# Expert down product of a decoder layer: both halves of the contraction as split products, with GpSimd making the low part of the second half

## The chip, the cores and the metric

The kernel runs on one core of a Trainium2 chip. The metric is the device time of one execution in microseconds. Times come from runs of the same program on the chip, and the rows below come from one further execution that was profiled.

## The reference

One decoder layer for 512 tokens of width 1024 in float32. It has a token mixer (a state-space branch and windowed attention, merged by gates, and an output product), and after it a mixture of experts, which is where the change lies:

```python
h2 = rmsnorm(x, norm_ffn)
gates = ...                      # top-1 of 4 groups, top-2 of its 4 experts: 16 experts in all
gu = jnp.einsum('nd,edf->nef', t, w_up)        # per expert: 1024 -> 512
g_part, u_part = jnp.split(gu, 2, axis=-1)
act = jax.nn.silu(g_part) * u_part * gates[..., None]
out = jnp.einsum('nef,efd->nd', act, w_down)   # per expert: 256 -> 1024
x = x + out
```

## The kernel before

Up to about 346 us of the profiled span the mixer and the router run. Then come the 16 experts, one after another. For each expert the kernel holds a list of up to 128 tokens. GpSimd gathers their rows from HBM (`gather`, line 674), TensorE transposes them (`turn_rows`, 2086), multiplies them by the up weights (`up`, 2100 to 2102), ScalarE and VectorE form the activation, TensorE transposes it (`turn_act`, 2112) and multiplies it by the down weights (`down_`). ScalarE scales the result by the token's gate out of PSUM (`rows_out`, 1011), and GpSimd adds the rows to the output in HBM with an accumulating indirect DMA (`add_rows`, 698; for the last four experts in two halves, 687).

Most products are split products. A float32 operand is written as a high part, which is rounded to `float32r` by a ScalarE copy, and a low part, the float32 operand less its high part, which VectorE computes. The product is then three `float32r` matmuls: high by high, high by low, low by high. The up product is split in full: 8 chunks of the contraction, three matmuls each, on two half weights (`high_up` at 977, `low_up` at 1596). The down product has a contraction of 256, that is two chunks `k`. Chunk 0 is split (2126 to 2128); its down weights get their high part on ScalarE (`high_down`, 997) and their low part on VectorE (`low_down`, 1642), its activations likewise (`turned_act` at 990, `low_act` at 1646). Chunk 1 is a plain float32 matmul (2121) from the unsplit activations (copied at 989) and the weights as they were loaded. The output has two column halves `h` of 512, each in its own PSUM bank.

The order on each engine is written out by hand. With `e` the expert whose up product is running:

- TensorE: up product of e, in the first six steps the small products that place two further token lists (2073), transposes of the activations of e-1, transposes of the rows of e+1, down product of e-1. In a down product the plain matmuls of both halves come first, then the three split matmuls of each half. The last expert's half 0 is finished before half 1 is begun.
- ScalarE: high part of the first up half of e+1, rows out of e-2, high down weights of e-1, high part of the second up half of e+1 (which waits until three halves back is used), transposed activations of e-1, tanh for e, high part of the rows of e+1.
- VectorE: list work (1578 to 1591) in the first steps, low part of the first up half of e+1, low down weights of e-1, low part of the second up half of e+1, low activations of e-1, low part of the rows of e+1 (1630), the activation of e (1636, 1638).
- GpSimd: gathers run ahead; before the gather of expert e comes the add of expert e-5. The gather of e waits until the rows of e-2 have been transposed. An add waits for the rows out of its own expert and for the landing of the add before it.
- SyncE loads up halves into a ring of 12 and down weights into 4 slots, expert e+3 after the down product of e-1 is done.

Of the kernel before, what the change touches and what calls it, by code (L numbers as in the profile page):

```python
# [6 lines left out]
F32 = mybir.dt.float32  # L7
# [17 lines left out]
def hybrid_layer(nc, x, norm_mix, w_in, lam_re, lam_im, log_dt, b_re, b_im, c_re, c_im, d_skip,  # L25
# [36 lines left out]
    with ExitStack() as ctx:  # L62
# [3 lines left out]
        def sem(name):  # L66
# [8 lines left out]
                     att=3 * 1024, v=TT * KW, kt=KVH * SEQ, rot=4 * SPC * CH // 2, ssm=max(SSM_FLOATS, 4 * DOWN + 6 * 256))  # L75
# [99 lines left out]
        at_high = [rounded(f"at_high{i}", "att", 1280 + 2 * D + 256 * i, [P, P]) for i in range(2)]  # L175
        at_low = [rounded(f"at_low{i}", "att", 1792 + 2 * D + P * i, [P, P]) for i in range(2)]
        dn_high = [rounded("dn_high", "att", 0, [P, D])] * (NE - 1) + [rounded("dn_high_last", "ga", 0, [P, D])]
        dn_low = [rounded(f"dn_low{s}", "ssm", s * DOWN, [P, D]) for s in range(4)]
# [126 lines left out]
        dn_high_done, dn_low_done, at_low_done = (sem(n) for n in ("dn_high_done", "dn_low_done", "at_low_done"))  # L305

# [288 lines left out]
        def _(g):  # L595
# [105 lines left out]

            for t in range(TT):
                g.wait_ge(h2_stored[t], 16)
            for e in range(NE):
                if e == 5:
                    g.wait_ge(x2_stored, 16 * TT)
                if e >= 5:
                    add_rows(e - 5)
                if e < 2:
                    g.wait_ge(first_idx, e + 1)  # L710
                elif e in LISTS:
                    g.wait_ge(idx_done, LISTS.index(e) + 1)
                gather(e)
            for e in range(NE - 5, NE):
                add_rows(e)

# [16 lines left out]
        def _(act):  # L733
# [252 lines left out]
            def turned_act(e):  # L986

                act.wait_ge(at_full, e + 1)
                act.activation(actT[e % 2][:, 1, :], sc[1][:, P:2 * P], ACT.Copy).then_inc(at_done, 1)
                act.activation(at_high[e % 2][:], sc[1][:, 0:P], ACT.Copy).then_inc(at_done, 1)  # L990

            def high_down(e):
# [4 lines left out]
                act.activation(dn_high[e][:], down[e % 4][:, 0, :], ACT.Copy).then_inc(dn_high_done, 1)  # L997
# [63 lines left out]
        def _(v):  # L1061
# [578 lines left out]
            def low_down(e):  # L1640
                v.wait_ge(dn_high_done, e + 1)
                tt(dn_low[e % 4][:], down[e % 4][:, 0, :], dn_high[e][:].bitcast(F32), ALU.subtract).then_inc(dn_low_done, 1)

            def low_act(e):
                v.wait_ge(at_done, 2 * (e + 1))
                tt(at_low[e % 2][:], sc[1][:, 0:P], at_high[e % 2][:].bitcast(F32), ALU.subtract).then_inc(at_low_done, 1)
# [50 lines left out]
        def _(pe):  # L1697
# [417 lines left out]
            def down_(e):  # L2115
                pe.wait_ge(at_done, 2 * e + 1)
                pe.wait_ge(down_loaded[e % 4], 16 * (e // 4 + 1))
                cols = [slice(h * 512, (h + 1) * 512) for h in range(2)]

                def plain(h):  # L2120
# [105 lines left out]
```

## Time and profile before

| | us |
|---|---|
| median of 3 runs | 535.05 |
| lowest and highest | 531.87, 536.57 |
| the profiled execution | 533.41 |
| its span in the trace | 531.6 |
| TensorE busy | 503.6 (95%) |
| VectorE busy | 385.2 (72%) |
| ScalarE busy | 296.8 (56%) |
| GpSimd busy | 146.7 (28%) |

PE is TensorE's matmuls, PEld its weight loads, DVE is VectorE, ACT is ScalarE, POOL is GpSimd. L with a number is a line of the kernel. Positions are microseconds from the start of the span. The names `arena_front` and `arena_back` are two large SBUF tensors in which most tiles lie, so a tile's name in a row is often that of the arena; the line says which it is. `m_both` are the two PSUM banks of the down product, `sc_both` holds the transposed activations, `tp` the transposed rows and, for the last expert, the down product.

### The profile page before, as it was taken

Reading aid. Unit: us, or ns where it says so; the run is one execution under the profiler, and the core shown is the slowest. Engines: PE = TensorE matmul, PEld = TensorE weight load, DVE = VectorE, ACT = ScalarE, POOL = GpSimd, SP = SyncE. Lnnn points to the kernel's source line nnn. Section 1 sums busy time; section 2 is a strip of 40 time slices with the busy share of each in tenths; the row PEclk is TensorE's granted clock in tenths of the full one; section 3 lists DMA queues with packets and bytes.
Section 4 is the critical chain, followed back from the end, with each engine's and each line's share of the span. In section 5 each row is a group of like instructions: output and inputs, shape, how many; then the busy total and the mean of one; then the engine's idle time right before and its main releaser. Section 6 shows DMA issues by size and latency. Waiting matters only on the chain.

```text
span 531.6 us, 7304 instructions
## 1 busy us (share of the span) xinstructions
PE 503.6 (95%) x2610; PEld 409.4 (77%) x2610; DVE 385.2 (72%) x609; ACT 296.8 (56%) x523; POOL 146.7 (28%) x188
## 2 busy tenths in 40 slices
PE   6999999898999999999999999779999999999992
PEld 4988787687777887778888888777878877777761
DVE  4889876989879658665758424578988888788740
ACT  6635143776676876632335102345677777787741
POOL 1229429294470000000000000032233223345344
PEclk9999999999999999999999999958999999999997
DMA  8660460222012220243587547579999999966433
GB/s 312 85 206 1 121 197 5 76 80 80 27 54 80 61 60 0 60 118 103 174 297 284 232 188 287 193 247 413 370 322 338 321 357 372 331 234 175 123 46 38
DMA packets 62774, 93.93 MB, mean 177 GB/s; under 512 B 14183, under 2 KB 45959, under 8 KB 62738
## 3 DMA queue, kind: packets, MB, share of 16 engines
q1 hardware_dynamic: 56304, 80.84, 44.2%
q0 software_dynamic: 5184, 8.41, 7.3%
q10 hardware_dynamic: 1250, 4.22, 2.0%
q8 instruction: 21, 0.34, 0.3%
q14 instruction: 15, 0.12, 0.1%
HBM read 88.19 MB, written 12.58 MB: 190 GB/s over the span
## 4 chain that ended last, share of the span: by engine, by line
PE 82%; DVE 9%; ACT 4%; DMA 2%; issue 1%; POOL 0%; SPq 0%; POOLq 0%; DVEq 0%; ACTq 0%
PE pj L1723 12%; PE pj L1725 11%; PE pj L1724 11%; PE pj L2100 6%; PE pj L2101 6%; PE pj L2102 6%; PE m_both L2121 5%; PE tp L2086 3%; DMA arena_front<-in_w_in_dram 1%; PE m_both L2126 1%; PE m_both L2128 1%; PE m_both L2127 1%; PE m_both L1723 1%; PE m_both L1725 1%; PE m_both L1724 1%
## 5 line engine op out<-in xcount | busy, mean ns | idle before, releaser
L1723 PE MATMUL pj<-h_high,split 128*128 128x512 f32 x192 | 76.6, 399 | 2.2 <-ACT arena_back L841 1.5
L1725 PE MATMUL pj<-h_high,split 128*128 128x512 f32 x192 | 74.9, 390 | 0.0
L1724 PE MATMUL pj<-h_low,split 128*128 128x512 f32 x192 | 74.8, 390 | 0.0
L1596 DVE TENSOR_TENSOR up_low<-arena_front,up_high 128x2048 fp32r<-128x2048 f32 x23 | 52.7, 2290 | 10.9 <-ACT up_high L977 10.9
L615 POOL TENSOR_TENSOR rstd<-ssq,half_col 128x1 f32<-128x1 f32 x8 | 4.4, 554 | 197.0 <-DVE ssq L1100 184.0
L2100 PE MATMUL pj<-up_high,xt_high 128*128 128x512 f32 x128 | 51.2, 400 | 0.9 <-DVE xt_low L1630 0.9
L2101 PE MATMUL pj<-up_low,xt_high 128*128 128x512 f32 x128 | 50.7, 396 | 0.0
L2102 PE MATMUL pj<-up_high,xt_low 128*128 128x512 f32 x128 | 50.6, 395 | 0.0
L977 ACT ACTIVATE up_high<-arena_front 128x2048 fp32r<-128x2048 f32 x23 | 44.3, 1929 | 10.5 <-PE pj L2102 9.4
L1723 PEld LDWEIGHTS pj<-h_high,split 128*128 128x128 f32 x192 | 36.1, 188 | 12.1 <-issue 3.3
L434 DVE TENSOR_TENSOR split<-arena_front,split 128x2048 fp32r<-128x2048 f32 (+1 forms) x20 | 41.9, 2095 | 4.6 <-ACT split L415 4.4
L415 ACT ACTIVATE split<-arena_front 128x2048 fp32r<-128x2048 f32 (+1 forms) x20 | 34.9, 1744 | 17.9 <-PE sc_both L1725 10.9
L698 POOL DMA_INDIRECT out_dram<-arena_back,idx_all x12 | 24.8, 2063 | 67.4 <-DMA out_dram<-arena_back,idx_all 42.8
L1725 PEld LDWEIGHTS pj<-h_high,split 128*128 128x128 f32 x192 | 36.0, 188 | 7.7
L1724 PEld LDWEIGHTS pj<-h_low,split 128*128 128x128 f32 x192 | 36.1, 188 | 7.0
L674 POOL DMA_INDIRECT arena_front<-h_rows,idx_all x16 | 27.4, 1714 | 35.9 <-PE tp L2086 21.5
L2100 PEld LDWEIGHTS pj<-up_high,xt_high 128*128 128x128 f32 x128 | 24.6, 192 | 6.3 <-DVE xt_low L1630 1.1
L2102 PEld LDWEIGHTS pj<-up_high,xt_low 128*128 128x128 f32 x128 | 24.6, 192 | 5.3
L2101 PEld LDWEIGHTS pj<-up_low,xt_high 128*128 128x128 f32 x128 | 24.6, 192 | 5.1
L2121 PE MATMUL m_both<-arena_back 128*128 128x512 f32 x60 | 28.2, 593 | 0.0
L1011 ACT ACTIVATE arena_back<-m_both,gate_all 128x512 f32<-128x512 f32 x30 | 19.0, 685 | 13.7 <-PE m_both L2128 13.7
L957 ACT ACTIVATE arena_back<-arena_back 128x512 f32<-128x512 f32 x8 | 5.0, 629 | 36.7 <-DVE arena_back L1123 36.7
(327 smaller groups left out, 1274.5 us busy)
## 6 DMA issues: line engine op xcount, KB each, us to landing
arena_front<-in_w_expert_up_dram SPq DMA_DIRECT2D x23, 1024.0 KB, 11.6
arena_back<-in_w_expert_down_dram SPq DMA_DIRECT2D x16, 1024.0 KB, 10.8
arena_front<-in_w_in_dram SPq DMA_DIRECT2D x12, 1024.0 KB, 5.5
arena_back<-in_w_expert_up_dram SPq DMA_DIRECT2D x9, 1024.0 KB, 13.0
arena_front<-in_w_out_dram SPq DMA_DIRECT2D x4, 1024.0 KB, 6.0
arena_back<-in_x_dram SPq DMA_DIRECT2D x4, 512.0 KB, 6.2
arena_front<-in_w_ssm_glu_gate_dram SPq DMA_DIRECT2D x8, 256.0 KB, 2.8
arena_front<-in_w_ssm_glu_val_dram SPq DMA_DIRECT2D x8, 256.0 KB, 3.3
```

The lines of the kernel that those rows point to most:

```text
L415: nc.scalar.activation(w_high[split_place(n)][:, 0:z], raw[n % 2][:, 0:z], ACT.Copy).then_inc(high_done, 1)
L434: eng.tensor_tensor(w_low[s][:, 0:z], raw[n % 2][:, 0:z], w_high[s][:, 0:z].bitcast(F32), ALU.subtract).then_inc(low_done, 1)
L674: g.indirect_dma_start(xg[e % 2], None, h2_rows, bass.IndirectOffsetOnAxis(idx_all[:, e:e + 1], 0), bounds_check=SEQ - 1, oob_is_err=False ...
L977: act.activation(up_high[i % 3][:], ring[i % NH], ACT.Copy).then_inc(up_high_done, 1)
L1596: tt(up_low[i % NH][:], ring[i % NH], up_high[i % 3][:].bitcast(F32), ALU.subtract).then_inc(up_low_done, 1)
L1723: pe.matmul(dst, sh, mh, start=first and i == 0, stop=False)
L1724: pe.matmul(dst, sh, ml, start=False, stop=False)
L1725: ins = pe.matmul(dst, sl, mh, start=False, stop=last and i == len(terms) - 1)
L2100: pe.matmul(pj[e % 2][:], xs[0], ws[0], start=k == 0, stop=False)
L2101: pe.matmul(pj[e % 2][:], xs[0], ws[1], start=False, stop=False)
L2102: ins = pe.matmul(pj[e % 2][:], xs[1], ws[0], start=False, stop=k == DC - 1)
L2121: pe.matmul(y_bank(e, h), actT[e % 2][:, 1, :], down[e % 4][:, 1, cols[h]], start=True, stop=False)
```

## The change

The second chunk of the contraction becomes a split product too. ScalarE makes a high part of its weights in two pieces of 512 columns, ahead of the high part of the first chunk, and both transposed activation chunks in one copy of 256 columns. VectorE's low activations cover both chunks. The low part of the second chunk's weights is made by GpSimd, in two pieces, each after the matching piece of ScalarE; on GpSimd's queue these subtractions for expert e-4 stand between the add of e-5 and the gather of e, and at the end between the adds. TensorE runs chunk 0 of both halves, then chunk 1, three `float32r` matmuls each; the plain matmuls are gone. The wait on the low activations now stands ahead of the third matmul, and each half's chunk 1 waits for its GpSimd piece. Buffers grow accordingly.

```diff
+        def dn_high(e, k, h):
+            cols = slice(h * 512, (h + 1) * 512)
+            if e == NE - 1:
+                return dn_last[:, k, cols]
+            return dn_second[h][:] if k else dn_first[:, cols]
...
+            def second_low(e):
+                for h in range(2):
+                    g.wait_ge(dn_second_high, 2 * e + h + 1)
+                    cols = slice(h * 512, (h + 1) * 512)
+                    g.tensor_tensor(dn_low[e % 4][:, 1, cols], down[e % 4][:, 1, cols], dn_high(e, 1, h).bitcast(F32), ALU.subtract
+                                    ).then_inc(dn_second_low, 1)
...
                 if e >= 5:
                     add_rows(e - 5)
+                if e >= 4:
+                    second_low(e - 4)
...
                 gather(e)
             for e in range(NE - 5, NE):
                 add_rows(e)
+                if e + 1 < NE:
+                    second_low(e + 1)
...
             def turned_act(e):
                 act.wait_ge(at_full, e + 1)
-                act.activation(actT[e % 2][:, 1, :], sc[1][:, P:2 * P], ACT.Copy).then_inc(at_done, 1)
-                act.activation(at_high[e % 2][:], sc[1][:, 0:P], ACT.Copy).then_inc(at_done, 1)
+                act.activation(at_high[e % 2][:], sc[1][:, 0:2 * P].rearrange("p (k n) -> p k n", k=2), ACT.Copy).then_inc(at_done, 2)
...
-                act.activation(dn_high[e][:], down[e % 4][:, 0, :], ACT.Copy).then_inc(dn_high_done, 1)
+                first = dn_last[:, 0, :] if e == NE - 1 else dn_first[:]
+                for h in range(2):
+                    act.activation(dn_high(e, 1, h), down[e % 4][:, 1, h * 512:(h + 1) * 512], ACT.Copy).then_inc(dn_second_high, 1)
+                act.activation(first, down[e % 4][:, 0, :], ACT.Copy).then_inc(dn_high_done, 1)
...
             def low_act(e):
                 v.wait_ge(at_done, 2 * (e + 1))
-                tt(at_low[e % 2][:], sc[1][:, 0:P], at_high[e % 2][:].bitcast(F32), ALU.subtract).then_inc(at_low_done, 1)
+                tt(at_low[e % 2][:], sc[1][:, 0:2 * P].rearrange("p (k n) -> p k n", k=2), at_high[e % 2][:].bitcast(F32), ALU.subtract
+                   ).then_inc(at_low_done, 1)
...
             def down_(e):
-                pe.wait_ge(at_done, 2 * e + 1)
-                pe.wait_ge(down_loaded[e % 4], 16 * (e // 4 + 1))
...
-                def plain(h):
-                    pe.matmul(y_bank(e, h), actT[e % 2][:, 1, :], down[e % 4][:, 1, cols[h]], start=True, stop=False)
...
+                pe.wait_ge(at_done, 2 * (e + 1))
+                if e and e < NE - 1:
+                    pe.wait_ge(y_scaled, e * 2)
+
+                def parts(h, k):
+                    if k:
+                        pe.wait_ge(dn_second_low, 2 * e + h + 1)
+                    else:
+                        pe.wait_ge(dn_low_done, e + 1)
+                    low = dn_low[e % 4][:, k, h * 512:(h + 1) * 512]
+                    pe.matmul(y_bank(e, h), at_high[e % 2][:, k, :], dn_high(e, k, h), start=k == 0, stop=False)
+                    pe.matmul(y_bank(e, h), at_high[e % 2][:, k, :], low, start=False, stop=False)
                     pe.wait_ge(at_low_done, e + 1)
+                    return pe.matmul(y_bank(e, h), at_low[e % 2][:, k, :], dn_high(e, k, h), start=False, stop=k == 1)
 
                 if e == NE - 1:
                     for h in range(2):
-                        plain(h)
-                        parts(h).then_inc(dn_full, 1)
+                        for k in range(2):
+                            ins = parts(h, k)
+                        ins.then_inc(dn_full, 1)
                     return
...
-                for h in range(2):
-                    plain(h)
-                parts(0)
-                parts(1).then_inc(dn_full, 1)
+                for k in range(2):
+                    for h in range(2):
+                        ins = parts(h, k)
+                ins.then_inc(dn_full, 1)
```

## Rows read from the trace of the kernel before

**Rows 1.** The page, busy time of TensorE over the span.
```profile
PE 503.6 (95%) x2610; PEld 409.4 (77%) x2610; DVE 385.2 (72%) x609; ACT 296.8 (56%) x523; POOL 146.7 (28%) x188
```

**Rows 2.** Busy time by stretch: first list step, a later one, a late step.
```profile
core 0: us, PE busy (x) PEld busy (x) DVE busy (x) ACT busy (x) POOL busy (x), PEclk, DMA share, GB/s
368.20:378.70 10.50, 10.50 (x53) 8.36 (x52) 10.43 (x18) 7.50 (x9) 1.45 (x2) 1.00 1.03 409
...
389.30:399.90 10.60, 10.60 (x54) 8.44 (x53) 9.29 (x14) 7.62 (x10) 3.70 (x2) 1.00 0.98 329
...
460.00:469.70 9.70, 9.70 (x46) 7.49 (x45) 7.91 (x9) 7.62 (x10) 4.55 (x3) 1.00 0.78 274
```

**Rows 3.** Timeline of TensorE, one late step: start us, us, instruction, count.
```profile
459.85 0.39 PE L2100 MATMUL pj<-up_high,xt_high 128*128 128x512 f32 x1
...
465.30 0.38 PE L2112 MATMUL sc_both<-ident,arena_back 128*128 128x128 f32 x2
...
466.47 1.88 PE L2121 MATMUL m_both<-arena_back 128*128 128x512 f32 x4
...
469.35 0.39 PE L2128 MATMUL m_both<-dn_high,at_low 128*128 128x512 f32 x1
469.58 0.39 PE L2100 MATMUL pj<-up_high,xt_high 128*128 128x512 f32 x1
```

**Rows 4.** Timeline of ScalarE, the same late step.
```profile
460.11 1.27 ACT L1011 ACTIVATE arena_back<-m_both,gate_all 128x512 f32<-128x512 f32 x2 [0.63 <-PE m_both L2128]
461.26 1.06 ACT L997 ACTIVATE dn_high<-arena_back 128x1024 fp32r<-128x1024 f32 x1
462.83 1.92 ACT L977 ACTIVATE up_high<-arena_back 128x2048 fp32r<-128x2048 f32 x1 [0.51 <-PE pj L2102]
465.71 0.28 ACT L989 ACTIVATE arena_back<-sc_both 128x128 f32<-128x128 f32 x1 [0.97 <-PE sc_both L2112]
```

**Rows 5.** Timeline of VectorE, the same late step.
```profile
462.35 1.23 DVE L1642 TENSOR_TENSOR dn_low<-arena_back,dn_high 128x1024 fp32r<-128x1024 f32 x1 [0.55 <-ACT dn_high L997]
464.78 2.29 DVE L1596 TENSOR_TENSOR up_low<-arena_back,up_high 128x2048 fp32r<-128x2048 f32 x1 [1.20 <-ACT up_high L977]
466.99 0.28 DVE L1646 TENSOR_TENSOR at_low<-sc_both,at_high 128x128 fp32r<-128x128 f32 x1
```

**Rows 6.** Timeline of GpSimd, adds in list steps and in late steps.
```profile
392.09 2.65 POOL L698 DMA_INDIRECT out_dram<-arena_back,idx_all  x1 [4.04 <-DMA out_dram<-arena_back,idx_all]
...
404.97 3.46 POOL L698 DMA_INDIRECT out_dram<-arena_back,idx_all  x1 [6.30 <-DMA out_dram<-arena_back,idx_all]
...
467.56 1.59 POOL L698 DMA_INDIRECT out_dram<-arena_back,idx_all  x1 [4.85 <-DMA out_dram<-arena_back,idx_all]
...
477.48 1.59 POOL L698 DMA_INDIRECT out_dram<-arena_back,idx_all  x1 [5.04 <-DMA out_dram<-arena_back,idx_all]
```

**Rows 7.** Timeline of GpSimd and VectorE where both subtract or multiply, in the mixer.
```profile
106.24 2.25 POOL L649 TENSOR_TENSOR arena_back<-arena_back 128x16 f32<-128x16 f32 x1
...
119.79 1.05 POOL L649 TENSOR_TENSOR arena_back<-arena_back 128x504 f32<-128x504 f32 x1
...
121.92 1.40 POOL L651 TENSOR_TENSOR arena_back<-arena_back 128x252 f32<-128x252 f32 x1
...
106.13 2.29 DVE L434 TENSOR_TENSOR split<-arena_front,split 128x2048 fp32r<-128x2048 f32 x1
...
122.70 2.78 DVE L434 TENSOR_TENSOR split<-arena_front,split 128x2048 fp32r<-128x2048 f32 x1
```

**Rows 8.** Groups by line over the expert stage: busy us, mean ns, idle before.
```profile
L983 ACT ACTIVATE xt_high<-tp 128x512 fp32r<-128x512 f32 x32 | 17.8, 622 | 7.6 <-PE tp L2086 7.6
...
L1029 ACT ACTIVATE arena_back<-pj 128x256 f32<-128x256 f32 x16 | 6.3, 392 | 0.8 <-PE pj L2102 0.8
```

**Rows 9.** Timeline of VectorE, low activations in the first list step.
```profile
375.95 0.28 DVE L1646 TENSOR_TENSOR at_low<-sc_both,at_high 128x128 fp32r<-128x128 f32 x1
```

**Rows 10.** Timeline of GpSimd, half adds of experts 14 and 15.
```profile
519.51 1.55 POOL L687 DMA_INDIRECT out_dram<-arena_back,idx_half  x1 [0.30 <-issue]
...
525.21 1.55 POOL L687 DMA_INDIRECT out_dram<-arena_back,idx_half  x1 [0.61 <-issue]
```

More of the change, by code:

```diff
@@ L74, in hybrid_layer @@
         sizes = dict(raw=2 * PIECE, pair=4 * PIECE, ht=2 * SLOT, uz=CT_ * 512, qy=4 * 512, gs=SLOT, ga=SLOT, u4=ST * CH,
-                     att=3 * 1024, v=TT * KW, kt=KVH * SEQ, rot=4 * SPC * CH // 2, ssm=max(SSM_FLOATS, 4 * DOWN + 6 * 256))
+                     att=3 * 1024, v=TT * KW, kt=KVH * SEQ, rot=4 * SPC * CH // 2, ssm=max(SSM_FLOATS, 4 * DOWN + 9 * 256))
         arena_at = (nc.sbuf_base + 31) // 32 * 32
@@ L173, in hybrid_layer @@
         actT = [part("att", 1280 + 2 * D + 256 * i, 256, k=2, n=P) for i in range(2)]
[L175 to L178, printed above, removed]
+        at_high = [rounded(f"at_high{i}", "att", 1280 + 2 * D + 256 * i, [P, 2, P]) for i in range(2)]
+        at_low = [rounded("at_low0", "att", 1792 + 2 * D, [P, 2, P]), rounded("at_low1", "ssm", 4 * DOWN + 6 * 256, [P, 2, P])]
+        dn_first = rounded("dn_high_first", "att", 0, [P, D])
+        dn_second = [rounded("dn_high_second0", "kt", 512, [P, 512]), rounded("dn_high_second1", "ssm", 4 * DOWN + 7 * 256, [P, 512])]
+        dn_last = rounded("dn_high_last", "ga", 0, [P, 2, D])
+        dn_low = [rounded(f"dn_low{s}", "ssm", s * DOWN, [P, 2, D]) for s in range(4)]
+        def dn_high(e, k, h):
[3 more added lines that the diff above has]
+            return dn_second[h][:] if k else dn_first[:, cols]
         th_e = [part("ssm", 4 * DOWN + 256 * i, 256) for i in range(2)]
@@ L305, in hybrid_layer @@
         dn_high_done, dn_low_done, at_low_done = (sem(n) for n in ("dn_high_done", "dn_low_done", "at_low_done"))
+        dn_second_high, dn_second_low = sem("dn_second_high"), sem("dn_second_low")
         pj_order, tp_order = [], []
@@ L1641, in low_down @@
                 v.wait_ge(dn_high_done, e + 1)
-                tt(dn_low[e % 4][:], down[e % 4][:, 0, :], dn_high[e][:].bitcast(F32), ALU.subtract).then_inc(dn_low_done, 1)
+                first = dn_last[:, 0, :] if e == NE - 1 else dn_first[:]
+                tt(dn_low[e % 4][:, 0, :], down[e % 4][:, 0, :], first.bitcast(F32), ALU.subtract).then_inc(dn_low_done, 1)
             def low_act(e):
                 v.wait_ge(at_done, 2 * (e + 1))
-                tt(at_low[e % 2][:], sc[1][:, 0:P], at_high[e % 2][:].bitcast(F32), ALU.subtract).then_inc(at_low_done, 1)
+                tt(at_low[e % 2][:], sc[1][:, 0:2 * P].rearrange("p (k n) -> p k n", k=2), at_high[e % 2][:].bitcast(F32), ALU.subtract
+                   ).then_inc(at_low_done, 1)
             low_rows(0)
```

8 lines of the change are left out of this document (removed).

## The prediction

> **What bounds the kernel now.** I read the page first: TensorE is busy for 503.6 us of 531.6 [rows 1]. The table of stretches tells the same of the expert stage alone [rows 2]: TensorE is never free in a step of 9.7 us (late steps) or 10.6 us (steps that also place token lists), at full clock, while VectorE works 7.9 to 10.4 us and ScalarE 7.5 to 7.6 us. So every TensorE microsecond saved is worth one, until another engine's chain is longer than the step. The timelines of one late step show these chains; I count t from the first matmul of its up product, 459.85 [rows 3]. TensorE: up product to t=5.45, transposes, down product from 6.62, next up product at 9.73. ScalarE: rows out, high part of the down weights, then at 2.98 the high part of the next up half [rows 4]. VectorE: that half's low part at 4.93 to 7.22, and only behind it the low part of the activations, 7.14 to 7.42 [rows 5]. GpSimd adds expert rows to the output, and each add waits for the one before to land [rows 6].
>
> **The change, part by part.** *TensorE.* The last matmul starts 0.23 before the next product, so a split product costs 0.232 us and the six of a down product 1.39; the plain ones took the other 3.11 - 1.39 = 1.72 us of it [rows 3]. Afterwards it is twelve at 0.232 = 2.78: 0.33 us less per expert, 5 us over 15. This is all the gain there is.
>
> *The low activations become urgent.* Plain products gave 1.72 us of cover; they need no low part. In the new order the third product already needs it: t = 6.62 + 0.46 = 7.08. VectorE has it at 7.42 at the earliest, and the tile is now 256 wide: between 0.28 us for 128 columns and 1.23 for 1024 [rows 5] that makes 0.41, done at 7.55. Ten products follow: 7.55 + 0.06 + 2.32 = 9.93. That alone turns 9.73 into 9.93: the saving is gone.
>
> *ScalarE.* Two copies of 128x512 come ahead of the old 128x1024 copy. One takes 0.62 us [rows 8]; as the two rows out of 0.69 take 1.27 together [rows 4], neighbours overlap by 0.1, so I take 0.5 of queue each, bounds 0.4 and 0.62. One transposed copy replaces two of 0.28 [rows 4]: 0.39 [rows 8], and TensorE's row transposes still cover it. So the old copy ends at t = 2.47 + 1.0 = 3.47, and the next up half, which had 0.51 us of slack before it, starts at 3.4 in place of 2.98. VectorE's low half follows it at once (before, it waited 1.20 for it), so everything moves by 0.42: low activations done at 7.97, down product done at 7.97 + 0.06 + 2.32 = 10.35. ScalarE's rows out of the next step wait for that product: this is a closed loop of 10.35 us against a TensorE step of 9.4.
>
> *GpSimd's subtractions.* The nearest row is 128x504 at 1.05 us [rows 7]. But a GpSimd instruction of 128x16 took 2.25 us beside a VectorE subtract of 2.29 that had begun 0.11 before it, and at 122.70 a VectorE subtract took 2.78, having begun while a GpSimd one of 121.92 to 123.32 still ran [rows 7]: each holds the other until its end. The Trainium skill ("GPSIMD Engine Reference", Key points) says that GpSimd's SBUF interfaces are shared with VectorE and contend when a VectorE instruction has two SBUF inputs; the trace agrees, and without that rule and those rows the sum would lack the next term. Bounds of a subtraction: 1.05 alone, 1.05 + 2.25 = 3.3 behind a VectorE half; it costs VectorE between 0 and 1.05. In a late step the first one is released when VectorE's down part ends (about 4.7) and runs to 5.75, while the up half is ready at 5.35: 0.4 more, or 0 where GpSimd comes later. I take 0.2. Late step: 10.35 + 0.2 = 10.55, +0.8 over 9.73, for nine steps **+7.2** (from +0.2 to +2.3 each, below).
>
> *Steps with lists.* Eight more small matmuls put the down product 0.87 later (10.60 against 9.73), so its third product comes at 7.95, level with the low activations at 7.97 to 8.37; the step is 10.35 to 10.75, against 10.60: no change of its own. In the first of them VectorE is busy for 10.43 of 10.50 us [rows 2] and its low activations begin at 375.95, as the down product starts [rows 9]; two subtractions hold it there for 1.05 each: **+2.1**.
>
> *What GpSimd's queue does.* The subtractions of expert E stand behind the add of expert E-1. An add has 1.59 us of its own, and took 3.46 at 404.97, where VectorE held its start [rows 6]. The next began 477.48 - 469.15 = 8.3 us after the one before had ended: landing and 0.8 us of start. Cadence 9.9 us unheld, up to 0.8 + 3.46 + 9.4 (the worst landing of the list steps) = 13.7. Before, this lag of up to 8 us cost nothing. Now it does once an add starts later than about t = 5.2, where the up half holds it: it ends at 9.0, the subtractions at 10.1 and 11.2, the last three products at 12. In four list steps I take 0.4 each, **+1.6** (0 to +1.7 each). The gather behind the subtractions is wanted two steps later, so it is free, and loads on SP wait on the down product as before and have three steps of cover.
>
> *The end.* Expert 15's subtractions stand behind both half adds of expert 14, the last of which starts at 519.51 [rows 10]. They would begin near 521.5 (expert 14 is 0.4 late) and end at 523.7 where TensorE finished near 523.0; its products, the copy out and two half adds in a row put the last issue near 526.9 in place of 525.21: **+2.1** with the 0.4 (bounds 0.8 and 4.5).
>
> Sum: 2.1 + 1.6 + 7.2 + 2.1 = 13.0. The profiled execution took 533.41 us (span 531.6 and 1.8 around it): 546.4. It lay 1.6 below the median of the three runs, 535.05, which I leave as spread: **546 us**.
>
> **Rivals.**
> *TensorE stays the bound (faster).* If VectorE and ScalarE shift earlier once TensorE is quicker, 15 x 0.33 = 5 us go, less 1 at the end: 529. For it: TensorE has no idle time now. Against: the low activations were ready only 8.34 - 7.42 = 0.9 us ahead of the first split product, and the 1.72 us of plain products before it are gone. It decides at an end of the low activations before t=7.1. Chance 0.09.
> *The stall eats the saving and no more.* Without ScalarE's delay and any holding, late steps are 9.93 and list steps 10.3: +1.8 - 1.2 + 1 = 535. It needs slack that the rows don't show ahead of the up half. Chance 0.19.
> *The add queue gates TensorE.* In list steps alone: 4 x 1.7 in place of 1.6, 551.6, chance 0.12. In late steps too, where a held add keeps itself late (12.0 against 9.73): 9 x 2.3 in place of 7.2, 565, chance 0.08. For it: adds already lag 7 us. Against: unheld, their cadence is below the new step of 10.5, so the lag shrinks.
> *Forecast* as summed: 0.52.
>
> **The numbers.** One per cent (5.4 us) is about what can be told from no change. Faster by more: 0.08 of the first rival. Within: the rest of it, and the second, 0.20. Slower: 0.72. The range runs from 534, the second rival's middle, to 558, the forecast's upper bounds and the add queue in the list steps; it leaves out the first rival, the last one, and half a tenth.
>
> **What would show it.** In the changed profile a late step of 10.3 to 10.8 us; TensorE idle 0.7 to 1.3 us ahead of the third split product, released by VectorE's low activations; ScalarE's up half ending near t=5.3; VectorE subtracts up to 3.3 us long, and GpSimd's of 1.05 to 3.3. If TensorE waits instead on the second half's low part, the add queue is the cause. If late steps are 9.4 the forecast is wrong; if 9.9, ScalarE had slack that I missed.

## The result and the profile after

The changed kernel takes 591.23 us (median of 4 runs, 590.04 to 592.47) against 534.89 of the kernel before (531.87 to 536.57): ratio 1.1057, 95% interval 1.1029 to 1.1086. The forecast was 546 in a range of 534 to 558: the sign was right, the size was not. The profiled execution has a span of 588.2 us, 56.6 more than before. The first up product starts 0.6 us earlier (356.48), the last expert's 52.3 us later (560.83 in place of 508.50), and from there to the end it is 27.3 us in place of 23.1. So nearly all of it lies in the 15 steps before the last expert: 204.4 us in place of 151.4.

The nine late steps took 9.73 us each before. Now two of them take 12.6 and 12.7 us, six 13.9 to 14.6, and the last, that of the up product of expert 14, 15.7. Busy time of one of each (columns: stretch, length, then busy us and instructions of TensorE, its weight loads, VectorE, ScalarE, GpSimd, granted clock, DMA share, GB/s) to set beside [rows 2]:

```profile
core 0: us, PE busy (x) PEld busy (x) DVE busy (x) ACT busy (x) POOL busy (x), PEclk, DMA share, GB/s
476.70:491.40 14.70, 12.02 (x48) 9.42 (x48) 11.06 (x9) 8.49 (x11) 7.23 (x4) 0.83 0.72 246
491.40:504.00 12.60, 10.69 (x48) 8.45 (x46) 9.02 (x8) 8.60 (x11) 6.53 (x4) 0.93 0.48 125
```

TensorE now has 1.9 to 2.7 us without work in such a step (4.0 in the last one), and the granted clock is no longer 1.00. The mean of 0.83 is made of stretches at the two levels, 2.4 GHz and 1.2 GHz; the end of the step below is at the lower one. These are the timelines of the same step, the one that starts at 476.74, engine by engine; they answer to [rows 3 to 6]. ScalarE (start, length, instruction, count, and in brackets idle time and its releaser):

```profile
478.16 1.15 ACT L1020 ACTIVATE dn_high_second<-arena_back 128x512 fp32r<-128x512 f32 x2
479.20 1.06 ACT L1021 ACTIVATE dn_high_first<-arena_back 128x1024 fp32r<-128x1024 f32 x1
480.15 1.91 ACT L999 ACTIVATE up_high<-arena_back 128x2048 fp32r<-128x2048 f32 x1
```

GpSimd in the same step, the add and the two new subtractions:

```profile
479.09 1.59 POOL L708 DMA_INDIRECT out_dram<-arena_back,idx_all  x1 [5.66 <-ACT arena_back L1035]
480.17 3.07 POOL L717 TENSOR_TENSOR dn_low<-arena_back,dn_high_second 128x512 fp32r<-128x512 f32 x2
```

VectorE in the same step:

```profile
480.29 4.04 DVE L1667 TENSOR_TENSOR dn_low<-arena_back,dn_high_first 128x1024 fp32r<-128x1024 f32 x1 [3.26 <-ACT dn_high_first L1021]
484.26 2.28 DVE L1620 TENSOR_TENSOR up_low<-arena_back,up_high 128x2048 fp32r<-128x2048 f32 x1
486.46 0.41 DVE L1671 TENSOR_TENSOR at_low<-sc_both,at_high 128x256 fp32r<-128x256 f32 x1
```

TensorE's down product in the same step:

```profile
484.48 0.47 PE L2152 MATMUL m_both<-dn_high_first,at_high 128*128 128x512 f32 x1 [0.94 <-DVE dn_low L1667]
484.79 0.40 PE L2153 MATMUL m_both<-dn_low,at_high 128*128 128x512 f32 x1
486.93 0.80 PE L2155 MATMUL m_both<-dn_high_first,at_low 128*128 128x512 f32 x1 [1.74 <-DVE at_low L1671]
487.52 0.63 PE L2152 MATMUL m_both<-dn_high_first,at_high 128*128 128x512 f32 x1
487.95 0.63 PE L2153 MATMUL m_both<-dn_low,at_high 128*128 128x512 f32 x1
```

Read them in this order. ScalarE is as forecast: two pieces in 1.15 us, then the first chunk until 480.26. GpSimd begins its two subtractions behind the add, at 480.17, and ends them at 483.24. VectorE's low down part, 1.23 us long in [rows 5], is released at 480.29 and takes 4.04: it ends at 484.33, 1.09 after GpSimd's end. It has stood still for both subtractions, all but the first 0.1 us or so. Its up half is ready on ScalarE at 482.06 and starts at 484.26, the low activations end at 486.87, and TensorE, which had waited 0.94 us for the low down weights already, waits 1.74 us for them. After that wait the matmuls follow each other every 0.43 us in place of 0.23: half the clock, through the rest of the down product and the first matmuls of the next up product, until 493.1.

The step of 15.7 us has the same cause in another place. There the pair meets the up half, which takes 5.52 us in place of 2.29, and TensorE waits 4.01 us at once for the low activations. VectorE's and GpSimd's timelines:

```profile
550.48 5.52 DVE L1620 TENSOR_TENSOR up_low<-arena_front,up_high 128x2048 fp32r<-128x2048 f32 x1 [0.58 <-ACT up_high L999]
550.80 3.05 POOL L717 TENSOR_TENSOR dn_low<-arena_back,dn_high_second 128x512 fp32r<-128x512 f32 x2
```

The adds themselves don't hold VectorE. In the kernel before, its low down part is 1.22 to 1.23 us long in all steps and its up half 2.28 to 2.29, also where an add runs beside them; it is the add that grows. VectorE's timeline of the kernel before beside the add at 404.97 of [rows 6], which took 3.46 us:

```profile
404.67 2.29 DVE L1596 TENSOR_TENSOR up_low<-arena_back,up_high 128x2048 fp32r<-128x2048 f32 x1 [0.81 <-ACT up_high L977]
```

### The profile page after: what moved, and what is told of

It reads as the page before. It is cut to its first block, busy times and chain, and to the rows that moved or that the text cites. A ratio compares the mean times of both kernels' runs of the same rounds, so it can differ in the third digit from the quotient of the medians.

```text
span 588.2 us, 7400 instructions
## 1 busy us (share of the span) xinstructions
PE 525.2 (89%) x2642; PEld 428.8 (73%) x2642; DVE 426.9 (73%) x609; ACT 311.1 (53%) x539; POOL 197.7 (34%) x220
## 4 chain that ended last, share of the span: by engine, by line
PE 57%; DVE 25%; ACT 11%; POOL 2%; issue 2%; DMA 1%; POOLq 0%; ACTq 0%; DVEq 0%
PE pj L1749 11%; PE pj L1751 10%; PE pj L1750 10%; DVE dn_low L1667 9%; DVE up_low L1620 6%; PE m_both L2155 4%; ACT arena_back L1035 3%; PE m_both L2152 3%; PE m_both L2153 2%; ACT dn_high_second L1020 2%; ACT dn_high_first L1021 2%; POOL out_dram L697 1%; PE m_both L1749 1%; PE m_both L1750 1%; PE sc_both L1750 1%
## 5 line engine op out<-in xcount | busy, mean ns | idle before, releaser
L1667 DVE TENSOR_TENSOR dn_low<-arena_back,dn_high_first 128x1024 fp32r<-128x1024 f32 x15 | 54.6, 3637 | 37.2 <-ACT dn_high_first L1021 37.2
L1620 DVE TENSOR_TENSOR up_low<-arena_front,up_high 128x2048 fp32r<-128x2048 f32 x23 | 55.7, 2422 | 1.2 <-ACT up_high L999 1.2
L2126 PE MATMUL pj<-up_high,xt_high 128*128 128x512 f32 x128 | 52.8, 412 | 0.9 <-DVE xt_low L1654 0.9
L684 POOL DMA_INDIRECT arena_front<-h_rows,idx_all x16 | 39.8, 2486 | 37.0 <-PE tp L2112 24.9
L717 POOL TENSOR_TENSOR dn_low<-arena_back,dn_high_second 128x512 fp32r<-128x512 f32 x30 | 48.0, 1872 | 1.3 <-ACT dn_high_second L1020 1.3
L708 POOL DMA_INDIRECT out_dram<-arena_back,idx_all x12 | 20.2, 1682 | 63.9 <-ACT arena_back L1035 63.9
L2155 PE MATMUL m_both<-dn_high_first,at_low 128*128 128x512 f32 x30 | 17.5, 583 | 25.9 <-DVE at_low L1671 25.9
L2155 PEld LDWEIGHTS m_both<-dn_high_first,at_low 128*128 128x128 f32 x30 | 7.4, 246 | 33.0 <-DVE at_low L1671 31.9
```

Of the source, the lines that this page charges most:

```text
L717: g.tensor_tensor(dn_low[e % 4][:, 1, cols], down[e % 4][:, 1, cols], dn_high(e, 1, h).bitcast(F32), ALU.subtract).then_inc(dn_second_low, 1)
L1620: tt(up_low[i % NH][:], ring[i % NH], up_high[i % 3][:].bitcast(F32), ALU.subtract).then_inc(up_low_done, 1)
L1667: tt(dn_low[e % 4][:, 0, :], down[e % 4][:, 0, :], first.bitcast(F32), ALU.subtract).then_inc(dn_low_done, 1)
L2126: pe.matmul(pj[e % 2][:], xs[0], ws[0], start=k == 0, stop=False)
L2155: return pe.matmul(y_bank(e, h), at_low[e % 2][:, k, :], dn_high(e, k, h), start=False, stop=k == 1)
```

## Experiments

Ratios are to the kernel before, on the same chip. The median of the kernel before was 533.3 to 534.9 us in the rounds that these runs come from, so a difference between the times of two experiments can be off by 1 to 2 us.

**1. GpSimd's subtractions cut to 4 columns.**

```diff
                     cols = slice(h * 512, (h + 1) * 512)
-                    g.tensor_tensor(dn_low[e % 4][:, 1, cols], down[e % 4][:, 1, cols], dn_high(e, 1, h).bitcast(F32), ALU.subtract
+                    cols = slice(h * 512, h * 512 + 4)
+                    g.tensor_tensor(dn_low[e % 4][:, 1, cols], down[e % 4][:, 1, cols], dn_high(e, 1, h)[:, 0:4].bitcast(F32), ALU.subtract
...
-                    low = dn_low[e % 4][:, k, h * 512:(h + 1) * 512]
+                    low = dn_low[e % 4][:, 0, h * 512:(h + 1) * 512]
```

> The changed kernel with each GpSimd subtraction cut from 512 columns to 4; all waits, copies and matmuls stay, the second chunk's low product reads the first chunk's low weights instead, so its output is not the reference's. Theory L (both GpSimd subtractions hold VectorE's low down part for 3 us, and the loop through the low activations carries that on): VectorE's low down part is back at 1.2 us, the step is my forecast loop of 10.3 to 10.6 us, 540 to 550 us in all, at full clock. Rival W (the wait on the low activations and ScalarE's two copies alone cost it, GpSimd little): 580 to 590 us, as the changed kernel.

The kernel leaves out the second chunk's low weights. Measured: 542.27 us, ratio 1.0166 (1.0140 to 1.0192). Some 48 of the 56 us are gone. Late steps are 10.42 to 10.45 us, where the closed loop of the prediction had 10.35, and the granted clock in them is 1.00 again. VectorE in such a step, by its timeline:

```profile
475.65 1.22 DVE L1668 TENSOR_TENSOR dn_low<-arena_back,dn_high_first 128x1024 fp32r<-128x1024 f32 x1 [1.82 <-ACT dn_high_first L1022]
477.45 2.29 DVE L1621 TENSOR_TENSOR up_low<-arena_front,up_high 128x2048 fp32r<-128x2048 f32 x1 [0.58 <-ACT up_high L1000]
479.66 0.42 DVE L1672 TENSOR_TENSOR at_low<-sc_both,at_high 128x256 fp32r<-128x256 f32 x1
```

TensorE at the wait on the low activations of that step:

```profile
480.13 0.50 PE L2156 MATMUL m_both<-dn_high_first,at_low 128*128 128x512 f32 x1 [0.78 <-DVE at_low L1672]
480.47 0.40 PE L2153 MATMUL m_both<-dn_high_first,at_high 128*128 128x512 f32 x1
```

The wait on the low activations is 0.78 us here, and the matmul pitch after it stays near 0.23.

**2. The second chunk's low part on VectorE, nothing on GpSimd.**

```diff
+                for h in range(2):
+                    v.wait_ge(dn_second_high, 2 * e + h + 1)
+                    cols = slice(h * 512, (h + 1) * 512)
+                    tt(dn_low[e % 4][:, 1, cols], down[e % 4][:, 1, cols], dn_high(e, 1, h).bitcast(F32), ALU.subtract
+                       ).then_inc(dn_second_low, 1)
```

> The changed kernel with the second chunk's low part made by VectorE in two pieces behind its first chunk, nothing on GpSimd. Theory L: VectorE has 1.2 us more work of its own in place of 3 us of holding; its up half starts at t=5.7, late steps 10.7 us, list steps 11; 545 to 555 us. Rival W: VectorE was not held, so 1.2 us more work makes it slower than the changed kernel, 595 us or more.

GpSimd's two calls of `second_low` are gone. Measured: 549.56 us, 1.0293 (1.0263 to 1.0324); late steps 10.95 to 10.99 (expected 10.7). More work for VectorE is some 41 us cheaper than the same work on GpSimd, so it is the holding and not the load that costs.

**3. Low activations last.** TensorE's down product runs its eight products that need only high activations first, then the four with the low ones; GpSimd as changed.

```diff
-                def parts(h, k):
+                def high_act(h, k):
...
+                def low_act_part(h, k):
                     pe.wait_ge(at_low_done, e + 1)
                     return pe.matmul(y_bank(e, h), at_low[e % 2][:, k, :], dn_high(e, k, h), start=False, stop=k == 1)
...
                 for k in range(2):
                     for h in range(2):
-                        ins = parts(h, k)
+                        high_act(h, k)
+                for h in range(2):
+                    for k in range(2):
+                        ins = low_act_part(h, k)
```

> The changed kernel with TensorE's down product in another order: the eight products that need only the high activations first, the four with the low activations last; GpSimd as changed. Theory L: the loop still has the 3 us of holding but 6 products (1.4 us) leave it, so full-clock steps go from 12.6 to 11.2, and fewer idle stretches mean fewer steps at half clock: 560 to 570 us. Rival W: the wait on the low activations is nearly all of the cost, so this is back near 535 to 540 us.

Measured: 566.78 us, 1.0618 (1.0583 to 1.0654). The time is in the range expected, by way of other steps: six of the nine late steps are 11.8, not 11.2 (the others 11.4, 12.7 and 12.8), since VectorE's low down part is held for longer here, 4.65 us, by its timeline:

```profile
491.88 4.65 DVE L1667 TENSOR_TENSOR dn_low<-arena_back,dn_high_first 128x1024 fp32r<-128x1024 f32 x1 [0.45 <-ACT dn_high_first L1021]
```

GpSimd's timeline beside it:

```profile
490.68 2.21 POOL L708 DMA_INDIRECT out_dram<-arena_back,idx_all  x1 [5.05 <-ACT arena_back L1035]
492.38 3.06 POOL L717 TENSOR_TENSOR dn_low<-arena_back,dn_high_second 128x512 fp32r<-128x512 f32 x2
```

VectorE asked 0.5 us before GpSimd's subtractions are shown to start, while the add was still running, and was let through at their end all the same.

**4. The kernel before with GpSimd subtractions that nobody needs.**

```diff
+            def extra(e):
+
+                g.wait_ge(dn_high_done, e + 1)
+                if e:
+                    g.wait_ge(extra_done, 2 * e)
+                for h in range(2):
+                    cols, other = slice(h * 512, (h + 1) * 512), slice((1 - h) * 512, (2 - h) * 512)
+                    g.tensor_tensor(spare[h][:], down[e % 4][:, 1, cols], down[e % 4][:, 1, other], ALU.subtract).then_inc(extra_done, 1)
```

> The kernel before with two GpSimd subtractions of 128x512 added per expert, at the place of the changed kernel, on the down weights, into a spare tile that nobody reads (SyncE waits for them before it reloads the slot). Theory L: VectorE's low down part grows from 1.2 to about 4 us; late steps have 0.9 us of cover on the low activations and 0.6 of idle time, list steps hardly any, so 550 to 560 us. Rival W: 535 to 537 us, no change.

Measured: 547.92 us, 1.0266 (1.0231 to 1.0301), a little under the expectation; the extra pair was there for the first 12 experts only. No wait and no data of the other engines depends on it except SyncE's reload, and it still costs 14.7 us: 11.8 to 12.0 us in the list steps after the first in place of 10.6. What it held was the up half rather than the low down part, 4.93 us in place of 2.29 where the pair began 0.27 before it (VectorE's timeline):

```profile
464.92 4.93 DVE L1610 TENSOR_TENSOR up_low<-arena_back,up_high 128x2048 fp32r<-128x2048 f32 x1 [1.22 <-ACT up_high L991]
```

**5. Experiment 2 with the low activations last.** The edits of 2 and 3 together.

> Second chunk's low part on VectorE and the four products with the low activations last, nothing on GpSimd. Theory L (loop through ScalarE, VectorE and the low activations): the loop of 10.97 us loses six products, 1.39: 9.6 us in late steps against 9.73 of the kernel before; list steps are bound by VectorE, about 10.6 to 10.8. 533 to 537 us, level with before. Rival V (VectorE's own work is the bound, not the loop): late steps stay near 10.5, 543 us or more.

Measured: 533.16 us, 0.9999 (0.9984 to 1.0015), as expected: late steps 9.60 to 9.63, list steps after the first 10.4 to 10.5. The loop is now a shade longer than TensorE's work.

**6. Experiment 1 with the low activations last.**

> As the run with GpSimd's subtractions cut to 4 columns (low product of the second chunk reads the first chunk's low weights, so the output is not the reference's), with the low activations last. Theory L: the loop of 10.43 loses 1.39 and is below TensorE's own 9.41, so late steps are 9.4 and list steps 10.3: the whole TensorE saving of 0.33 us per expert shows, 528 to 530 us. Rival W (something else in the new order costs as much as it saves): 533 to 535 us.

Measured: 540.23 us, 1.0138 (1.0100 to 1.0177). Both theories missed. List steps after the first are 10.25 as theory L had them and five of the late steps 9.4 to 9.8, but four of the late steps are 11.35. There TensorE waits for GpSimd. First GpSimd's timeline of one of them:

```profile
466.05 3.03 POOL L708 DMA_INDIRECT out_dram<-arena_back,idx_all  x1 [6.72 <-DMA out_dram<-arena_back,idx_all]
468.56 0.89 POOL L718 TENSOR_TENSOR dn_low<-arena_back,dn_high_second 128x4 fp32r<-128x4 f32 x2
```

TensorE in the same step:

```profile
469.37 0.50 PE L2153 MATMUL m_both<-dn_high_second,at_high 128*128 128x512 f32 x1 [1.68 <-POOL dn_low L718]
```

The add waited 6.72 us for the landing of the one before, then fell into VectorE's up half (465.32, 2.29 us) and took 3.03 us in place of 1.59; the tiny subtractions stand behind it. This is the third rival of the prediction, the add queue, and it comes up only where the step is shorter than the adds' cadence. In the changed kernel it does not: there the adds wait for ScalarE's rows.

**7. TensorE's idle time filled.** Ten more matmuls per expert in the changed kernel.

```diff
+                def keep_busy(n):
+                    for _ in range(n):
+                        pe.matmul(y_bank(e, 1), at_high[e % 2][:, 0, :], dn_high(e, 0, 0), start=True, stop=True)
...
+                    if k == 0 and h == 0:
+                        pe.wait_ge(dn_high_done, e + 1)
+                        keep_busy(3)
...
+                    if k == 0 and h == 0:
+                        keep_busy(7)
```

> The changed kernel with ten more matmuls of 128x512 per expert in the down product's idle time, three ahead of the wait on the low down weights and seven ahead of the wait on the low activations; they write the second half's bank, which is overwritten by its own first product. Theory Q (after an idle stretch the clock falls, and steps of 14 to 15.7 us are steps of 12.6 at half clock for a while): all late steps at 12.6 to 12.9, granted clock back near 0.98, 572 to 580 us. Rival: the long steps have another cause, and the time stays at 590 us or grows by up to 35 (ten matmuls in 15 steps).

Measured: 578.05 us, 1.0824 (1.0797 to 1.0851). More matmuls, 13 us less. Eight of the nine late steps are 12.57 to 12.62 and the last 13.70 (in place of 15.70), and the granted clock is 1.00 from 371.5 to 562.6 us. Busy time by a stretch of one step's length (columns as above):

```profile
470.00:482.60 12.60, 12.24 (x58) 9.62 (x57) 10.73 (x10) 8.50 (x11) 7.24 (x5) 1.00 0.82 284
```

**8. GpSimd's subtractions after VectorE's low down part.**

```diff
+                g.wait_ge(dn_low_done, e + 1)
                 for h in range(2):
```

> The changed kernel with GpSimd's subtractions waiting until VectorE's low down part of that expert is done. Theory B (both GpSimd subtractions hold whatever VectorE subtract comes in their time): the low down part takes 1.2 us, and the next up half is held instead, 4 to 5 us; steps stay at 12 to 12.8 and the time at 580 to 592 us. Theory A, of the prediction (the two engines take turns, one GpSimd subtraction of about 1.3 us lets VectorE through): 570 us or less, with no VectorE subtract over 3.6 us.

Measured: 557.01 us, 1.0425 (1.0380 to 1.0470). Theory A holds in eight of the nine late steps, 11.07 to 11.11. VectorE's up half in its timeline:

```profile
484.73 2.94 DVE L1621 TENSOR_TENSOR up_low<-arena_front,up_high 128x2048 fp32r<-128x2048 f32 x1 [0.58 <-ACT up_high L1000]
```

GpSimd beside it:

```profile
481.72 1.59 POOL L708 DMA_INDIRECT out_dram<-arena_back,idx_all  x1 [2.81 <-ACT dn_high_second L1021]
484.23 4.58 POOL L718 TENSOR_TENSOR dn_low<-arena_back,dn_high_second 128x512 fp32r<-128x512 f32 x2 [0.92 <-DVE dn_low L1668]
```

The first subtraction starts with GpSimd idle, VectorE asks 0.50 us later and is held by 0.66, and then the second subtraction waits for VectorE: the pair takes 4.58 us. The engines take turns here, as the prediction had it. The last late step is 14.99 us, and there theory B holds. Its low down part is done before the pair's turn in the queue comes, so the pair follows the half adds directly; the up half takes 5.52 us, and TensorE waits 4.01, as in the changed kernel:

```profile
517.96 5.52 DVE L1621 TENSOR_TENSOR up_low<-arena_front,up_high 128x2048 fp32r<-128x2048 f32 x1 [0.58 <-ACT up_high L1000]
518.27 3.05 POOL L718 TENSOR_TENSOR dn_low<-arena_back,dn_high_second 128x512 fp32r<-128x512 f32 x2
```

**9. GpSimd's subtractions ahead of the add.**

```diff
+                if e >= 4:
+                    second_low(e - 4)
                 if e >= 5:
                     add_rows(e - 5)
-                if e >= 4:
-                    second_low(e - 4)
...
             for e in range(NE - 5, NE):
-                add_rows(e)
                 if e + 1 < NE:
                     second_low(e + 1)
+                add_rows(e)
```

> The changed kernel with GpSimd's two subtractions put ahead of the add of the expert before, so that they begin as soon as ScalarE's high parts are there (t=2 and 2.5) and not behind an add. Theory L: they end near t=4.5, hold VectorE's low down part by about 1.2 us in place of 3, and the step is 10.4 + 1.1 = 11.2 to 11.5 us without half clock: 555 to 562 us. Rival S (what counts is GpSimd's work as such, wherever it stands): 585 us or more.

Measured: 552.07 us, 1.0331 (1.0302 to 1.0361), 3 us under the range of theory L; late steps 10.74 to 10.78, VectorE's low down part 2.21 in its timeline:

```profile
463.50 2.21 DVE L1667 TENSOR_TENSOR dn_low<-arena_back,dn_high_first 128x1024 fp32r<-128x1024 f32 x1 [1.82 <-ACT dn_high_first L1021]
```

GpSimd's pair beside it:

```profile
462.08 2.54 POOL L717 TENSOR_TENSOR dn_low<-arena_back,dn_high_second 128x512 fp32r<-128x512 f32 x2 [2.11 <-ACT dn_high_second L1020]
```

The same work in another place of the queue costs 39 us less.

**10. The same with the low activations last.**

> The same with the products of the low activations last. Theory L: the loop of 11.2 to 11.5 loses 1.39, so late steps are 9.8 to 10.1 us, list steps 10.6 to 10.8 (VectorE has 9.35 us of its own and 1.2 of holding); 535 to 540 us. If the subtractions get through before VectorE asks, late steps are TensorE's 9.41 and the time 530.

Measured: 543.84 us, 1.0180 (1.0155 to 1.0204), over the range expected: eight of the nine late steps 10.03 to 10.06, but list steps after the first are 11.2 to 11.5. In late steps VectorE is held twice, its low down part (1.79 us) and its up half (3.27), and in list steps it has hardly any idle time for that.

**11. Low part on VectorE, first chunk's high part first, low activations last.** Experiment 5 with this on ScalarE:

```diff
+                act.activation(first, down[e % 4][:, 0, :], ACT.Copy).then_inc(dn_high_done, 1)
                 for h in range(2):
                     act.activation(dn_high(e, 1, h), down[e % 4][:, 1, h * 512:(h + 1) * 512], ACT.Copy).then_inc(dn_second_high, 1)
-                act.activation(first, down[e % 4][:, 0, :], ACT.Copy).then_inc(dn_high_done, 1)
```

> Second chunk's low part on VectorE, low activations last, and ScalarE's high part of the first chunk ahead of the second chunk's two. Theory L: VectorE's low down part starts at t=2.5 in place of 3.4 and its two pieces of 0.6 us fill what was idle time, so the loop is shorter than TensorE's 9.41: late steps 9.4, list steps 10.3 to 10.5; 528 to 531 us, 0.5 to 1% faster than the kernel before. Rival V (VectorE's work per step is the bound): as without this, 533 us.

Measured: 532.53 us, 0.9969 (0.9945 to 0.9992). Late steps are 9.38 to 9.39, the whole of TensorE's saving, and the last copy out starts at 518.57 in place of 523.14. But the span is only 1.2 us shorter: the half adds of the last experts wait for each other, as GpSimd's timeline of the last two shows:

```profile
521.50 1.55 POOL L697 DMA_INDIRECT out_dram<-arena_back,idx_half  x1 [1.51 <-DMA out_dram<-arena_back,idx_half]
524.02 1.55 POOL L697 DMA_INDIRECT out_dram<-arena_back,idx_half  x1 [0.97 <-DMA out_dram<-arena_back,idx_half]
```

**12. The same with half adds from expert 10 on**, and **14. the kernel before with only that** as its control.

```diff
-    HALVED = LISTS[-3]
+    HALVED = LISTS[-4]
```

> The last one (low part on VectorE, first chunk's high part first, low activations last) with the adds in two halves from expert 10 on in place of 12. There TensorE ended its work 4.8 us earlier than in the kernel before, but the span was only 1.2 us shorter, since the adds of experts 12 to 15 waited for each other's landing. Theory G (the gain was given back in the queue of adds): with the half adds two experts earlier the queue has caught up by the end; span 527 to 528, 528.5 to 530 us, 0.7 to 1.1% faster than the kernel before. Rival: half adds cost more descriptors and the time stays at 532.5.

> The kernel before with the adds in halves from expert 10 on, as a control of the run with VectorE. There the last adds wait for ScalarE's rows, not for each other, so nothing changes: 533 to 535 us by both theories; 530 or less would say that the halves alone are the gain.

Measured: 532.24 us, 0.9951 (0.9933 to 0.9969), and 534.03, 0.9996 (0.9979 to 1.0013). The adds are again released by ScalarE at the end (GpSimd's timeline of experiment 12):

```profile
521.09 1.55 POOL L697 DMA_INDIRECT out_dram<-arena_back,idx_half  x1 [3.07 <-ACT arena_back L1031]
522.95 1.55 POOL L697 DMA_INDIRECT out_dram<-arena_back,idx_half  x1 [0.30 <-issue]
```

The gain, half a per cent, is less than the 0.7 to 1.1 expected. In this profile the first six steps of the expert stage take 0.8 us more in sum than in experiment 11, and the last down product, behind 1.38 and 0.53 us of idle time as there, runs at half rate for most of its length, some 1.6 us more; in experiment 11 it ran at 0.23 us per matmul. TensorE's timeline of it here:

```profile
516.76 0.64 PE L2153 MATMUL tp<-dn_high_last,at_high 128*128 128x512 f32 x1 [0.53 <-ACT at_high L1007]
517.19 0.63 PE L2154 MATMUL tp<-dn_low,at_high 128*128 128x512 f32 x1
```

Its interval overlaps that of experiment 11, so it is not shown that the earlier half adds are worth anything; by its ratio it is the fastest version here.

**13. GpSimd's subtractions in eight pieces of 128 columns.**

```diff
-                    g.tensor_tensor(dn_low[e % 4][:, 1, cols], down[e % 4][:, 1, cols], dn_high(e, 1, h).bitcast(F32), ALU.subtract
-                                    ).then_inc(dn_second_low, 1)
+                    for q in range(4):
+                        cols = slice(h * 512 + q * 128, h * 512 + (q + 1) * 128)
+                        ins = g.tensor_tensor(dn_low[e % 4][:, 1, cols], down[e % 4][:, 1, cols],
+                                              dn_high(e, 1, h)[:, q * 128:(q + 1) * 128].bitcast(F32), ALU.subtract)
+                    ins.then_inc(dn_second_low, 1)
```

> The changed kernel with each GpSimd subtraction of 512 columns made in four of 128 columns, in the same place. Theory B (what follows back to back on GpSimd's queue behind an add holds VectorE until the last of it): VectorE's low down part stays at 4 us or more and the time at 588 to 600 us. Theory A (the engines take turns by the instruction): a low down part waits for one or two pieces, 1.5 to 2.2 us, the rest lies between VectorE's subtracts, and the time falls to 550 to 570 us.

Measured: 592.44 us, 1.1095 (1.1054 to 1.1136), as the changed kernel. But the sum hides two kinds of steps. In nine of them (14.2 to 15.3 us) theory B holds. VectorE's low down part in the timeline of one:

```profile
475.16 4.44 DVE L1670 TENSOR_TENSOR dn_low<-arena_back,dn_high_first 128x1024 fp32r<-128x1024 f32 x1 [3.41 <-ACT dn_high_first L1024]
```

GpSimd's pieces beside it:

```profile
475.03 4.86 POOL L719 TENSOR_TENSOR dn_low<-arena_back,dn_high_second 128x128 fp32r<-128x128 f32 x8
```

VectorE stands for some 3.2 us through a run of short instructions, so the holding does not end with the instruction that was running. In the other five, four list steps and the last late one (11.0 to 11.9 us), theory A holds: in all of them but the first list step the pieces follow an add just as directly, and no VectorE subtract is held for over 0.3 us. The last late step is the one to set beside the changed kernel's, since VectorE asked 0.3 us before GpSimd in both; VectorE's up half and GpSimd's eight pieces:

```profile
551.01 2.29 DVE L1623 TENSOR_TENSOR up_low<-arena_front,up_high 128x2048 fp32r<-128x2048 f32 x1 [0.58 <-ACT up_high L1002]
551.32 5.21 POOL L719 TENSOR_TENSOR dn_low<-arena_back,dn_high_second 128x128 fp32r<-128x128 f32 x8
```

With two long pieces the up half took 5.52 us, with eight short ones 2.29.

## Why the prediction was wrong

*What held.* TensorE's saving is as computed: 9.73 - 9.39 = 0.34 us a step once nothing else is in its way (experiment 11), forecast 0.33. The coverage of 1.72 us that the plain products gave, and the closed loop through rows out, ScalarE's copies, the up half and the low activations, are as computed too: 10.43 against 10.35 (experiment 1), and taking the six products out of it works as it should (experiment 5). ScalarE's pieces cost 1.04 of queue, forecast 1.0.

*The step that failed: "GpSimd's subtractions", "I take 0.2".* The rule of turns let VectorE go after one subtraction and put that mostly where VectorE was idle. It also had VectorE's low down part go first and GpSimd's first piece wait for its end, at t = 4.7. In the changed kernel the pair is there 0.12 us before VectorE, at t = 3.43, and VectorE's low down part is held for the pair, 4.04 - 1.23 = 2.8 us in the step shown; this part stands ahead of the up half and the low activations on the loop. Some 0.6 of the 2.8 fall in idle time ahead of the up half (0.58 in experiment 1), the rest makes 12.6 out of 10.43. By runs: 578.05 with the clock kept up less 542.27 without the subtractions is 36 us, 2.4 a step, where the sum had 0.2 and its upper bound 1.05 (the fillers' own cost is in the 36). A piece also takes about 1.27 us, not 1.05. The bound was wrong in kind: it was the length of one GpSimd instruction, since in [rows 7] each had held the other for one instruction at most, and no row showed GpSimd's subtractions behind an add.

*What the sum left out: the clock.* I had seen the granted clock at 1.00 in all steps and priced idle time on TensorE at its length. With 0.94 and 1.74 us of idle time in one down product, the matmuls after it ran at half rate. Experiment 7 gives its price: 591.2 - 578.1 = 13 us, net of what the fillers cost. The Trainium skill ("TensorE: Matmul & The Clock Gate", Part 1) says that a hardware monitor sets the clock by how busy TensorE has lately been; the trace agrees in that the fall came after idle time. It did not come in every step: where a down product of the changed kernel had waited 0.7 to 1.0 and then 1.7 us the clock fell each time, where it had waited 0.3 or less and then 1.7 us it did not (the step from 491.36, with 0.17 and 1.74, ran its down product at 0.23 us per matmul).

*The other terms.* The nine late steps took 38.8 us more than before, where the sum had 7.2, and the four later list steps 12.3, where it had 1.6. The first list step took 13.2 us in place of 10.7, +2.4 where the sum had 2.1, and that agreement is in part luck. VectorE was held there twice by 1.1 us, in turns, as forecast, but TensorE waited only 0.92 us for it; the step also began at half clock (366.8 to 370.2), as it did in experiment 11, where GpSimd has no subtractions and the step took 12.0. The end, from the last expert's up product on, took 4.2 us longer than before, forecast 2.1 with bounds to 4.5: TensorE waited 1.6 us there for GpSimd's low part of expert 15, and its last products ran at half rate. The other list steps, 12.5 to 14.8 us, have the same two causes as the late ones, not the add queue.

*The rivals.* Experiment 1 is the forecast's own loop without GpSimd's part. "The stall eats the saving" is near experiment 5 in time alone (533 us, with late steps of 9.6 and not 9.93), "TensorE stays the bound" became true only in experiment 11, and the add queue showed itself in experiment 6, not in the changed kernel. None of them had the holding in it.

*Not settled.* That GpSimd's pair holds VectorE is shown; what lets VectorE through is not. Where the pair of 512 columns starts from an idle GpSimd the engines take turns (experiments 8 to 10, and the first list step of the changed kernel). Where it follows an add directly, VectorE waits for all of it in all steps of the changed kernel and of experiment 3 in which it asks before the second subtraction, even if VectorE asked first; experiment 8 has both cases in one run. But in experiment 13 the pieces follow an add in thirteen steps, and VectorE was let through in four of them, so the add in front is not enough by itself. The records show one more thing that goes with the add: behind it GpSimd's two subtractions overlap (1.83 and 1.82 us long, the second 1.25 after the first, and so also at 574.01, where VectorE runs nothing), and from an idle GpSimd they overlap by 0.05 us at most. Whether it is this that keeps VectorE out was not tested; the step from 415.98 in experiment 13, where the pieces overlap and VectorE was held by 0.3 us, does not fit it. Experiment 9 does not decide it either: VectorE was held 1.0 us there, but it asked only when the second subtraction was running.

## What to carry to other kernels

Before work is moved to GpSimd, look at what VectorE does at that moment: a run of GpSimd tensor instructions can cost VectorE its whole length (here mostly where it followed an indirect add in the queue), and if VectorE's work lies on a closed loop, every microsecond is on the path once per step. When instructions that need no late operand are replaced, count what they covered: putting the products that need the late operand last (six products later here) bought 24 us in the changed kernel and 16 with VectorE. A saving on the busiest engine has to be followed to the last DMA: of 4.6 us that the copies out came earlier, 1.2 reached the end.

## What the runs showed of the hardware

- A VectorE subtract of 128x1024 (1.22 us alone) took 4.03 to 4.67 us beside GpSimd's pair of subtractions in the changed kernel and one of 128x2048 (2.29 alone) 5.52, where the pair followed an add; in experiment 8, where the pair started from an idle GpSimd, VectorE's 128x2048 took 2.94 and the pair 4.58, in place of 2.54 in a row.
- GpSimd's subtraction of 128x512 with a `float32r` result took 1.27 to 1.30 us, two in a row 2.54 (experiments 8 and 9).
- An indirect add of 1.59 us took 3.03 where a VectorE subtract was running at its start (experiment 6).
- In the changed kernel a down product ran at a pitch of 0.43 us per matmul after waits of 0.94 and 1.74 us, and another at 0.23 after 0.17 and 1.74. The last down product, behind idle stretches of 1.38 and 0.53 us both times, ran at 0.23 in experiment 11 and for most of its length at 0.43 in experiment 12.
